# Gate tables of a retrieval layer: one-hot products on TensorE replaced by indirect transfers that add into a cleared table in HBM

## The reference, cut to what matters

```python
q = (hf @ w_pq).reshape(M, PEER_HEADS, 2, PEER_HALF)
s1 = jnp.einsum('mhd,hnd->mhn', q[:, :, 0], sub_keys[0])
s2 = jnp.einsum('mhd,hnd->mhn', q[:, :, 1], sub_keys[1])
v1, i1 = lax.top_k(s1, 16)
v2, i2 = lax.top_k(s2, 16)
cand_s = v1[..., :, None] + v2[..., None, :]
cand_i = i1[..., :, None] * 128 + i2[..., None, :]
top_s, top_pos = lax.top_k(cand_s, 16)          # over the 256 pairs
idx = jnp.take_along_axis(cand_i, top_pos, axis=-1)
gate = jax.nn.softmax(top_s, axis=-1)
# for each token, over 8 heads and 16 picks:
act = gelu(expert_u[idx] . x)
y = sum(act * gate * expert_v[idx])
```

## Time and profile before

| | |
|---|---|
| runs | 4403.39, 4393.67, 4390.5 us; median 4393.67 us |
| profiled execution | 4389.36 us |
| its span, first to last instruction | 4387.6 us |
| mean granted TensorE clock | 0.959 |
| PE / DVE / ACT / POOL busy | 4089.7 / 2734.7 / 1549.1 / 1969.2 us |
| moved by DMA | 693.34 MB |

### The profile page before, as it was taken

How to read it: one execution, slowest core, us unless ns; L and a number is a source line. 1 busy time by engine, 2 the same in 40 slices (tenths; PEclk the granted TensorE clock), 3 DMA queues, 4 the chain that set the end, 5 groups by cost and what they waited for, 6 DMA issues and landing times.

```text
span 4387.6 us, 64423 instructions
## 1 busy us (share of the span) xinstructions
PE 4089.7 (93%) x19814; PEld 3376.1 (77%) x19814; DVE 2734.7 (62%) x5853; ACT 1549.1 (35%) x2469; POOL 1969.2 (45%) x1210
## 2 busy tenths in 40 slices
PE   7978888999999999999889888889999999999997
PEld 5776666888888887888766766668888888878886
DVE  4456323176868678888754562232768686688886
ACT  3424333333333333333334243433333333333333
POOL 4340333344343427777443413333443434377773
PEclk9988888999999999999999888899999999999999
DMA  3200121144353539999622012211444535399995
GB/s 125 87 1 20 67 96 55 68 145 141 131 196 126 202 126 338 333 338 343 225 98 87 1 30 76 78 68 68 144 138 151 177 144 185 138 343 339 341 333 219
DMA packets 232649, 693.34 MB, mean 158 GB/s; under 512 B 30544, under 2 KB 75696, under 8 KB 224816
## 3 DMA queue, kind: packets, MB, share of 16 engines
q1 hardware_dynamic: 134448, 444.88, 28.6%
q0 software_dynamic: 45888, 138.58, 8.2%
q10 hardware_dynamic: 52160, 107.98, 6.7%
HBM read 588.53 MB, written 102.81 MB: 158 GB/s over the span
## 4 chain that ended last, share of the span: by engine, by line
PE 55%; issue 26%; POOL 8%; DVE 3%; ACT 2%; PEld 1%; POOLq 1%; DVEq 1%; ACTq 1%; DMA 0%; PEldq 0%
PE PS L478 15%; PE PS L479 15%; PE PS L480 15%; POOL u_lo L1935 6%; POOL w_lo L1874 2%; PE PS L935 1%; PE PS L657 1%; PE PS L643 1%; PE PS L850 1%; ACT junk L972 1%; PE PS L895 1%; PE PS L661 1%; PE PS L532 1%; PE PS L472 1%; PE PS L860 1%
## 5 line engine op out<-in xcount | busy, mean ns | idle before, releaser
L1935 POOL TENSOR_TENSOR u_lo<-u_raw,u_hi 128x1024 fp32r<-128x1024 f32 x256 | 623.4, 2435 | 971.7 <-ACT u_hi L1284 971.7
L478 PE MATMUL PS<-h_hi,u_hi 128*128 128x512 f32 x2048 | 806.1, 394 | 2.2 <-POOL u_lo L1935 1.1
L479 PE MATMUL PS<-h_lo,u_hi 128*128 128x512 f32 x2048 | 797.4, 389 | 0.0
L480 PE MATMUL PS<-h_hi,u_lo 128*128 128x512 f32 x2048 | 797.2, 389 | 0.0
L1874 POOL TENSOR_TENSOR w_lo<-wring,w_hi 128x512 fp32r<-128x512 f32 (+1 forms) x352 | 467.4, 1333 | 600.0 <-ACT w_hi L991 596.1
L478 PE MATMUL PS<-v_hi,g_hi 128*128 128x512 f32 x1536 | 601.5, 392 | 22.8 <-DVE g_lo L1831 22.8
L1284 ACT ACTIVATE u_hi<-u_raw 128x1024 fp32r<-128x1024 f32 x256 | 271.2, 1060 | 947.9 <-PE PS L480 889.6
L479 PE MATMUL PS<-v_lo,g_hi 128*128 128x512 f32 x1536 | 600.3, 391 | 0.0
L480 PE MATMUL PS<-v_hi,g_lo 128*128 128x512 f32 x1536 | 600.1, 391 | 0.0
L1365 ACT ACTIVATE v_hi<-v_raw 128x1024 fp32r<-128x1024 f32 x256 | 271.6, 1061 | 560.8 <-PE PS L480 551.0
L1953 POOL DMA_INDIRECT v_row<-in_expert_v,row_index x256 | 381.6, 1491 | 165.3 <-DVE X L1841 107.4
(11 more groups left out here) (330 smaller groups left out, 6928.0 us busy)
## 6 DMA issues: line engine op xcount, KB each, us to landing
u_raw<-in_expert_u SPq DMA_DIRECT2D x256, 512.0 KB, 3.3
v_raw<-in_expert_v SPq DMA_DIRECT2D x256, 512.0 KB, 6.8
wring<-in_weights SPq DMA_DIRECT2D x42, 2048.0 KB, 8.5
acts_dram<-act_ring ACTq DMA_DIRECT2D x256, 256.0 KB, 2.0
saved<-acts_dram SPq DMA_DIRECT2D x64, 768.0 KB, 11.3
gates_dram<-gstage ACTq DMA_DIRECT2D x16, 2048.0 KB, 7.6
gates<-gates_dram SPq DMA_DIRECT2D x64, 512.0 KB, 6.5
crow_all<-crow_dram ACTq DMA_DIRECT2D x8, 512.0 KB, 6.0
```

The costliest lines, as they stand in the source:

```text
L478: mm(bank_ap, a_hi, b_hi, start=first, stop=False)
L479: mm(bank_ap, a_hi, b_lo, start=False, stop=False)
L480: return mm(bank_ap, a_lo, b_hi, start=False, stop=final)
L1935: g.tensor_tensor(u_lo[:, slot, :], u_raw[:, slot, :], u_hi[:, slot, :].bitcast(f32), ALU.subtract).then_inc(ulo_ready, 1)
```

## The change

The gate tables of blocks 1 to 3 are all kept in `gates_dram` and are no longer made by products.

- SP clears the three tables (3 x 8 MB) from a small tile of zeros, after the mixer's eighth weight load is issued. DVE fills the tile of zeros in the projection stage, and ACT waits for the clearing before the squares of the second norm.
- DVE computes for each pick its place in the table (`gate_place`) and its gate (`gate_value`).
- POOL issues for each block 128 indirect transfers that add one value for each of 128 tokens to HBM, in groups of 16 (one head), and waits before each group until all earlier ones have landed. That makes 384 transfers and 24 groups a layer. Picks of one head are distinct, so no group adds twice to one place.
- `u_lo` moves from POOL to DVE (`low_u`), at fixed places inside the picks: 15 tiles for each token block, of which 9 before the gates are ready for Exp, and the last 66 behind the picks. The ring of `u` has four slots instead of two. The order of the picks is 1, 2, 3, 0.
- PE's S_PICK is 128 tiles and nothing else. ACT's is rounds of four tiles, with the Exp after round 2, 6, 10 and 13.
- In S_PEER three tables are loaded for every four tiles (768 KB instead of 512 KB), and DVE multiplies in one instruction. The first four `v` tiles are loaded ahead of the first gates, and the first gates wait for all 384 transfers.

```diff
 # SP
+                sp.wait_ge(zeros_ready, 1)
+                for t in range(NG):
+                    sp.dma_start(gates_dram[t].rearrange("p i c -> p (i c)").rearrange("p (r n) -> p r n", n=2 * P),
+                                 zeros.rearrange("p (o n) -> p o n", o=1).to_broadcast([P, NEXP_HI // 2, 2 * P])).then_inc(gates_zeroed, 16)
                 with nc.sync.Fori(MIX_GROUPS // 2, N_PAIRS) as q:
...
-                with nc.sync.Fori(0, NEXP_HI // 2) as j:
-                    for slot in range(2):
-                        load_u(j * 2 + slot, slot)
+                for slot in range(2):
+                    load_u(slot, slot)
+                sp.wait_ge(stage_done, 4 * (S_PQ + 1))
+                for slot in range(2, U_RING):
+                    load_u(slot, slot)
+                with nc.sync.Fori(1, NEXP_HI // U_RING) as j:
+                    for slot in range(U_RING):
+                        load_u(j * U_RING + slot, slot)
...
-                sp.wait_ge(picks_ready, NG)
-                sp.wait_ge(spread_done, 4 + (NG - 1) * HOTS)
-                sp.wait_ge(gates_out, 16 * GATE_CHUNKS * (NG - 1))
+                sp.wait_ge(index_ready, 1)
+                for r in range(QUAD):
+                    load_v(r, r)
                 for slot in range(2):
                     sp.wait_ge(act_saved[slot], 16 * QUAD // 2)
+                sp.wait_ge(gates_scattered, l * (16 * NG * P) + 16 * NG * P)
                 load_gated(0, 0)
-                for r in range(QUAD):
-                    load_v(r, r)
 # PE, S_PICK
+                with nc.tensor.Fori(0, NEXP_HI // U_RING) as j:
+                    for slot in range(U_RING):
+                        expert_acts(j * U_RING + slot, slot)
 # DVE
+                def low_u(n):
+                    dve.wait_ge(uhi_ready, n + (U_RING + 1))
+                    slot = n % U_RING
+                    v.tensor_tensor(u_lo(slot), u_raw(slot), u_hi(slot).bitcast(f32), ALU.subtract).then_inc(ulo_ready, 1)
...
-                for t in range(NT):
+                n_low = 2
+                for i, t in enumerate(PICK_ORDER):
                     for k in range(16):
                         top16(scores[:, t, k * P:(k + 1) * P], rest[:, k % 4, :], top[:, k, :], topi[:, k, :])
+                        if k % 3 == 2:
+                            low_u(n_low)
+                            n_low += 1
...
                         top16(cand, cand2, best[:, h, :], besti[:, h, :])
+                        if h % 2 == 1:
+                            low_u(n_low)
+                            n_low += 1
...
-                    v.tensor_tensor(gate, gate, along(rinv[:, 0:PH], TOPK), ALU.mult)
+                    v.tensor_tensor(gate_value[:, t - 1, :].rearrange("p (h k) -> p h k", k=TOPK), gate, along(rinv[:, 0:PH], TOPK), ALU.mult)
+                    v.tensor_scalar(digitf[:, 0, :], picked[:, 0, :], float(P), own_place, ALU.mult, ALU.add)
+                    dve.drain()
+                    v.scalar_tensor_tensor(digitf[:, 0, :], picked[:, 1, :], float(NEXP_HI * P), digitf[:, 0, :], ALU.mult, ALU.add)
+                    dve.drain()
+                    v.tensor_scalar(gate_place[:, t - 1, :], digitf[:, 0, :], float((t - 1) * P * NEXP_HI * P), None, ALU.add)
                     dve.drain().then_inc(picks_ready, 1)
-                    dve.wait_ge(pickT_stored, t)
-                    with v.Fori(0, HOTS // 4) as j:
...
+                for n in range(n_low, NEXP_HI):
+                    low_u(n)
 # POOL, S_PICK
-                with g.Fori(1, NEXP_HI // 2) as j:
-                    for slot in range(2):
-                        split_u(j * 2 + slot, slot)
+                for t in range(NG):
+                    pool.wait_ge(picks_ready, t + 1)
+                    for h in range(PH):
+                        done = t * PH + h
+                        if done:
+                            pool.wait_ge(gates_scattered, l * (16 * NG * P) + 16 * TOPK * done)
+                            pool.sem_inc(scatter_room, 1)
+                        for k in range(h * TOPK, (h + 1) * TOPK):
+                            g.indirect_dma_start(gates_by_place, bass.IndirectOffsetOnAxis(gate_place[:, t, k:k + 1], 0),
+                                                 gate_value[:, t, k:k + 1], None, compute_op=ALU.add).then_inc(gates_scattered, 16)
```

More of the change, by code:

```diff
@@ L262, in trunk_kernel, with ring_of, u_raw, u_hi @@
         scores = area("scores", 18432, NT, 16 * P)
[L264 to L270, removed]
+        u_raw_0, u_hi_0, u_lo_0 = area("u_raw", 10240, 2, DC * P), area_r("u_hi", 12288, 2, DC * P), area_r("u_lo", 14336, 2, DC * P)
+        u_raw_2, u_hi_2, u_lo_2 = area("u_raw2", 26624, 2, DC * P), area_r("u_hi2", 28672, 2, DC * P), area_r("u_lo2", 30720, 2, DC * P)
+        def ring_of(first, second, slot):
+            return first[:, slot] if slot < 2 else second[:, slot - 2]
+        def u_raw(slot):
+            return ring_of(u_raw_0, u_raw_2, slot)
+        def u_hi(slot):
+            return ring_of(u_hi_0, u_hi_2, slot)
+        def u_lo(slot):
+            return ring_of(u_lo_0, u_lo_2, slot)
         act_ring = area("act_ring", 16384, 2, SEQ)
@@ L351, in trunk_kernel @@
         row_gathered = [sem(f"row_gathered{r}") for r in range(GATHERS)]
-        gates_out = lsem("gates_out")
         act_saved = [lsem("act_saved0"), lsem("act_saved1")]
-        u_loaded = [lsem("u_loaded0"), lsem("u_loaded1")]
+        u_loaded = [lsem(f"u_loaded{r}") for r in range(U_RING)]
         v_loaded = [lsem(f"v_loaded{r}") for r in range(QUAD)]
@@ L1302, in gates_store @@
[L1302 to L1305 removed]
+                        act.wait_ge(act_saved[slot % 2], half_n * 16)
+                    act.wait_ge(act_done, n + (U_RING + 1))
+                    fn(act_ring[:, slot % 2, :], PS[:, slot, :], ACT.Gelu_apprx_tanh).then_inc(gelu_done, 1)
@@ new lines, in gelu_saved, with acts_round @@
+                    act.wait_ge(gelu_done, n + (U_RING + 1))
+                    act.dma_start(acts_dram[bass.ds(n, 1)].rearrange("i p n -> (i p) n"), act_ring[:, slot % 2]).then_inc(act_saved[slot % 2], 16)
+                def acts_round(j, first=False, final=False):
+                    for slot in range(U_RING):
+                        if not final:
+                            split_u(j * U_RING + (slot + U_RING), j + 1, slot)
+                        gelu_saved(j * U_RING + slot, j * 2 + slot // 2, slot, first and slot < 2)
@@ L1307, in _, with gate_exps @@
+                def gate_exps(i):
+                    act.wait_ge(gate_diff, i + 1)
+                    fn(picked[:, 2, :], picked[:, 2, :], ACT.Exp).then_inc(gate_exp, 1)
                 split_u(0, 0, 0)
@@ L1312, in _ @@
                 stage_end(act, l, S_PQ)
-                for slot in range(2):
-                    acts_step(0, slot, first=True)
-                with nc.scalar.Fori(1, U_FIRST // 2 - 1) as j:
-                    for slot in range(2):
-                        acts_step(j, slot)
-                act.wait_ge(gate_diff, 1)
-                fn(picked[:, 2, :], picked[:, 2, :], ACT.Exp).then_inc(gate_exp, 1)
-                for slot in range(2):
-                    acts_step(U_FIRST // 2 - 1, slot)
@@ new lines, in _ @@
+                for slot in range(2, U_RING):
+                    split_u(slot, 0, slot)
+                rounds = [(2 + i * LOWS_OF_BLOCK + LOWS_TO_BEST + U_RING - 1) // U_RING for i in range(NT)]
+                acts_round(0, first=True)
+                at = 1
+                for i in range(NT):
+                    with nc.scalar.Fori(at, rounds[i]) as j:
+                        acts_round(j)
+                    gate_exps(i)
+                    at = rounds[i]
+                with nc.scalar.Fori(at, NEXP_HI // U_RING - 1) as j:
+                    acts_round(j)
@@ L1736, in _ @@
                 split_x(XP_PQ, h_lo, hT, h_hi)
+                def low_u(n):
+                    dve.wait_ge(uhi_ready, n + (U_RING + 1))
+                    slot = n % U_RING
+                    v.tensor_tensor(u_lo(slot), u_raw(slot), u_hi(slot).bitcast(f32), ALU.subtract).then_inc(ulo_ready, 1)
+                for n in range(2):
+                    low_u(n)
                 stage_end(dve, l, S_PQ)
```

167 lines of the change are left out of this document (42 added, 125 removed).

## The result

The changed kernel takes 4643.29 us (median of four runs, 4640.01 to 4648.09) against 4394.06 us before in the same session. The ratio is 1.0565, with an interval of 1.0546 to 1.0583: 5.6% slower. I had predicted 4268 us and a range of 4250 to 4580. So forecast and range are both wrong, on the side of rival 1.

What follows compares the result with a forecast made beforehand. PE was taken to bound S_PICK and S_PEER. From 4389.4 us, 2 x 64.1 off for PE's S_PICK and 2 added for clearing gave 4263; the runs' median lies 4.3 higher, so 4268 us, range 4250 to 4580.

Steps and rivals of the forecast that it cites:

- rival 1: End of S_PICK: POOL ends last at 1.95 us a transfer, S_PICK ends at 1725, kernel 4578 us; chance 0.33.
- the price of an adding transfer: POOL's transfers cost what gathers cost: 1.53, later 1.42 us each, 26.2 and 24.5 us a group.
- Cover of 27 us: End of S_PICK: POOL ends at 1551, PE at 1578, transfers hidden with 27 us to spare, 0.07 us a transfer.
- threshold of 84: POOL's extra time from which the gain is eaten: 84 us, 0.22 us a transfer more than forecast.
- The sub-rival: POOL: adds read two sources, so the 0.94 us issue grows by half, kernel about 4590 us; chance 0.15 of 0.33.
- The wait at each group: POOL: a group of 16 ends when its last transfer lands, 2.9 us after issue, and 0.3 to the next.
- PE's work: S_PICK: PE needs 696.3 us without one-hot products, plus 23.7 lost to late low parts: 720.0, gaining 64.1 us a layer.
- DVE's blocks: S_PICK: a token block on DVE with 15 low parts of 1.2 us takes 86.7 us against PE's 81.6.
- rival 3: S_PICK: POOL holds DVE up as before, 63 us lost instead of 24, kernel 4346 us; chance 0.06.
- S_PEER: Loads for four tiles grow from 5376 to 5632 KB, 353 GB/s; PE stays the limit and nothing is lost.
- Rival 4: S_PEER is limited by its transfers, kernel 4316 us; chance 0.06.
- Clearing: Stores that zero the tables meet ACT's decay rows: zero to 10 us a layer, taken as 1.

Runs made afterwards that it cites:

- hidden transfers: The changed kernel without its adding transfers (4277.34 us), or with plain stores (4279.72 us) or gathers (4275.99 us) in their place.

## Why the prediction was wrong, step by step

**The step that failed** is the price of an adding transfer: "the nearest rows are its gathers of the same 128 indices", 1.53 and 1.42 us from start to start, 26.2 and 24.5 us a group. Gathers and plain stores do what it says: with plain stores POOL's first transfer starts at 953.1 and the last group is out at 1553.5, 600.4 / 24 = 25.0 us a group. An add costs 0.59 us more at issue (1.546 against 0.958). It took 2.13 us with its share of all waits and (1770.4 - 953.4) / 24 = 34.0 us a group. POOL ended S_PICK at about 1773 instead of 1551, 222 us late. Some 7 of these are its later start, 953.4 instead of 946.0; the rest is the price.

My own formula then comes within 31 us. Cover of 27 us, 222 late: 4268 + 2 x (222 - 27) = 4658, and 16 more for the first gates, 4674; measured 4643. Of the 31 us, 21 are cover: PE ended at 1588.5 and not at 1578, so each layer had some 37 us and not 27. The first gates cost DVE 4.4 us of visible wait, and some is given back. PE waited for its first `g_lo` for 192.9 us against 5.0 with plain stores, but in the 20 us after its restart it was busy for 16.7 against 12.4, and its S_PEER, from first to last product, takes 529 us against 534.5. Likely the `v` tiles had long been there; no run isolates this.

**Rival 1** is what came about, with its mechanism and its place; 222 us are well past its threshold of 84. Its price was too low, 32.5 us a group against 34.0, because I bounded the add by the gather beside a busy DVE, 1.95 us. The range ended there. I wrote that no row showed what an add costs, and yet took the nearest row for a bound. The sub-rival with half as much again at issue (0.94 to 1.41) was close in size: the factor is 1.546 / 0.944 = 1.64 against a gather. Its mechanism is not shown.

The Trainium skill (Collectives: The Full Stack, The bandwidth ceiling) says of the add in a ring collective that it reads two sources and takes two read descriptors a piece, where a copy takes one. The traces show packets and not descriptors: 144 for an add and 32 for a store, 4.5 times as many and not twice. So they neither bear the page out nor refute it. They do show that the price at issue does not go by the number of packets: at half the elements an add makes 80 packets instead of 144, and its surplus over a store falls only from 0.59 to 0.52 us (medians).

**The wait at each group.** I took 2.9 us from issue to use and 0.3 to the next, 1.7 us more than between two transfers. The rows have POOL stand for 2.1 instead of 0.3 us where nothing else runs, and up to 4.7 beside transfers. Taking the wait away gave 2.1 us a group. Right in kind, and 0.4 us small.

**PE's work.** PE's S_PICK lasts from 865.05 to 1588.5, 723.4 us; forecast 720.0. That is 27.1 us over the 696.3 of its 128 tiles, forecast 23.7, and all of it lies before 1210. From 865.05 to 1210 PE stands for 19 us; the other 8 are products that lie further apart, 326.0 us for 1403 of them where 5.44 a tile would make 318. The granted clock stays at 0.99 in these gaps, as forecast from the earlier trace rows.

**DVE's blocks.** The places' first instruction in the three blocks:

```profile
951.53 0.28 DVE L1771 TENSOR_SCALAR digitf<-picked,places 128x128 f32<-128x128 f32 x1
1038.34 0.30 DVE L1771 TENSOR_SCALAR digitf<-picked,places 128x128 f32<-128x128 f32 x1
1128.71 0.28 DVE L1771 TENSOR_SCALAR digitf<-picked,places 128x128 f32<-128x128 f32 x1
```

86.8 and 90.4 us apart; forecast 86.7. The low part of `u` takes 1203/1226/1274 ns (shortest, median, longest) beside POOL's transfers and 1203/1225/1228 with none, forecast 1.2 us. DVE held up by POOL, rival 3, is out. The Trainium skill (SBUF — State Buffer, Who interferes with whom) has a DVE instruction with two SBUF inputs and a GpSimd one that reads SBUF lock each other out, by order of issue. The trace shows POOL's half of it. In layer 1, 33 of the 49 adds that start while a low part runs take over 1.66 us, but only 3 of the 93 during which a low part starts; transfers reach 3.6 us beside the picks' widest instruction of two inputs (L1743, 2.3 us). DVE's half does not show: no low part takes over 1.274 us, whichever came first.

**S_PEER.** 355 GB/s with PE busy for 100 of 100 us, at a DMA share of 0.98; forecast 353 and no loss. With hidden transfers the stage takes 534.5 us against 533.6 before. Rival 4 is out, though the margin is thin.

**Clearing.** The decay rows wait as I feared, 3.5 us at the first use, and about 3 us a layer go by the times, with the reserve above. I took 1 from bounds of 0 and 10.

**The sum without the failed term** was 4268; the kernel with hidden transfers has 4276 to 4280. S_PICK is 3.4 us and S_PEER 1 us a layer longer than I took, together 9 us.

**What stays open.** Beside the picks the adds stand further apart than alone: 256.6 / 116 = 2.21 us against 182 / 90 = 2.02. Part is DVE: of the 384 adds of layer 1, the 193 that overlap no DVE instruction all take 1.54 to 1.57 us, and 41 of the 43 over 1.66 overlap one of over 0.9 us. This is small, 0.08 us an add on the mean, and plain stores have it too (1.071 on the mean against 0.952 at the least). Single idle gaps of 1.8 to 4.7 us within a group also come where nothing is waited for in the profile, even while DVE and PE stand. They go by the count of transfers and not by time: in both layers they stand behind the same ones, the 113th, 226th and 339th, with adds, stores and gathers alike, and with adds of 128 elements also behind the 60th, 120th, 180th, 300th and 360th (and the 240th in the run without waits; elsewhere a group ends there). The gap at 1084.48 above is behind the 60th; with plain stores the first is behind the 113th:

```profile
1134.27 0.96 POOL L1912 DMA_INDIRECT gates_dram<-gate_value,gate_place  x1 [4.92 <-issue]
```

Adds of 64 elements have only those at multiples of 113, stores of 64 none. In the changed kernel the gaps sum to 19 us a layer; what makes them is not shown. Why an add costs 0.42 us more at issue before any element is counted is not shown either.

## What to carry to other kernels

Price a transfer that does arithmetic as a kind of its own. If no row shows it, the nearest row is not a bound; here the add took 1.6 times the gather, so a range for an unpriced instruction that is issued 384 times on one queue should hold a factor of two. When work moves to a queue with 27 us to spare behind it, write down the price a piece at which the cover ends (here 0.07 us) and ask what supports the figure to that precision.

Equal places need not be added by the transfer. If stores are ordered anyway, prefix sums on an engine with idle time make the last store right, and the cheap kind of transfer does the rest: 80.6 us on DVE took 200 us off POOL's 818.

## What the runs showed of the hardware that I had not expected

- An indirect transfer of 128 single floats issued by GpSimd takes 0.944 us as a gather, 0.958 as a store and 1.546 as an add at the median, with 0.30 us to the next each time. For 64 floats it is 0.892 as a store and 1.412 as an add. By a line through the two points, an estimate, 0.82 us of the store and 1.24 of the add are a fixed price.
- In the DMA queue such an add makes 144 packets and a store 32; with 64 floats it is 80 and 32.
- The wait for the landing of a group is the same for adds and plain stores: 2.0 and 2.1 us at the least, up to 4.8 beside other traffic.
- POOL's indirect transfers pause for 1.8 to 4.9 us behind the 113th, 226th and 339th of a layer, and with adds of 128 floats also behind each 60th that does not end a group.
- An adding transfer that POOL starts while DVE's low part (two inputs, 1.2 us) runs is mostly stretched (33 of 49 in layer 1); one that started first seldom is (3 of 93). DVE's low part keeps its time either way.
- With PE idle for 193 us the granted clock went to 0.50, the lower level. In the first 20 us after the restart it was 0.92 on the mean, and 1.00 in the next 20. With plain stores, after a gap of 5 us, it was 0.75 in PE's first 20 us, with PE busy for 12.4 of them, and 1.00 in the next 20.
